# Two hi parts and the x reload moved in the middle of the MLP; in the second block one sum moved to GpSimd and the rotations set apart between heads

## The reference

```python
    # end of the first block (4096 hidden features)
    h = _rmsnorm(x, ln_mlp_g[l])
    x = x + jnp.square(jax.nn.relu(h @ w_mlp_up[l])) @ w_mlp_down[l]

    # second block
    h = x @ w_in
    x_q, x_kv, k_rope_raw, gate_a, u_pool, gate_b = jnp.split(h, splits, axis=-1)
    y_a = mla_branch(x_q, x_kv, k_rope_raw, ...) * jax.nn.silu(gate_a)
    y_b = pool_branch(u_pool, pool_w, pool_scale) * jax.nn.silu(gate_b)
    x = layer_norm(alpha * x + jnp.concatenate([y_a, y_b], axis=-1) @ w_out, ln_g, ln_b)

    # in mla_branch: 4 heads, 128 + 64 (rotated) features a query, latents of 512 and 256
    q = (rms_norm(x_q, q_norm_g) @ w_uq).reshape(B, S, MLA_HEADS, QK_DIM)
    q_nope, q_rope = q[..., :QK_NOPE_DIM], q[..., QK_NOPE_DIM:]
    q_rope = apply_rope(q_rope, cos[:, :, None, :], sin[:, :, None, :])
    kv = (rms_norm(x_kv, kv_norm_g) @ w_ukv).reshape(B, S, MLA_HEADS, QK_NOPE_DIM + V_HEAD_DIM)
    k_rope = apply_rope(k_rope_raw, cos, sin)
```

## Time and profile before

| what | value |
|---|---|
| three runs | 2297.06, 2299.01, 2300.14 us (median 2299.01) |
| profiled execution | 2299.54 us |
| its span, first to last instruction | 2297.7 us |
| mean granted TensorE clock | 0.995 |
| busy: TensorE / VectorE / GpSimd / ScalarE | 2235.4 / 1694.5 / 1195.4 / 837.3 us |
| DMA | 272.50 MB, mean 119 GB/s |

### The profile page before, as it was taken

The page is one execution under the profiler, slowest core; times in us unless marked ns, Lnnn a source line. Parts: engine busy times, 40 slices in busy tenths (PEclk is TensorE's granted clock), DMA queues, the critical chain, the costliest instruction groups (busy, mean ns, idle before and its releaser), DMA issues. The chain is left out here.

```text
span 2297.7 us, 29211 instructions
## 1 busy us (share of the span) xinstructions
PE 2235.4 (97%) x10722; PEld 1849.6 (80%) x10722; DVE 1694.5 (74%) x2037; ACT 837.3 (36%) x1165; POOL 1195.4 (52%) x895
## 2 busy tenths in 40 slices
PE   7999999999999999999999999899999999999998
PEld 5678888888888899787878888788888777778886
DVE  7899999986778354446587766677777866578777
ACT  4312243123334256213343333444343434344423
POOL 4136553333323266334478988998886678400140
PEclk9999999999999999999999999999999999999999
DMA  4121123633332422444234445654442212441231
GB/s 155 37 83 64 64 92 106 169 138 113 108 128 92 129 66 65 156 146 165 83 135 153 151 171 189 256 193 156 147 156 101 70 37 92 131 152 49 65 110 73
DMA packets 93733, 272.50 MB, mean 119 GB/s; under 512 B 8800, under 2 KB 25320, under 8 KB 87080
## 3 DMA queue, kind: packets, MB, share of 16 engines
q1 hardware_dynamic: 76544, 206.86, 26.8%
q10 hardware_dynamic: 17064, 63.99, 7.9%
HBM read 186.13 MB, written 83.90 MB: 118 GB/s over the span
## 5 line engine op out<-in xcount | busy, mean ns | idle before, releaser
L1247 PE MATMUL pair<-actA,w_hi 128*128 128x512 f32 x2016 | 624.5, 391 | 2.1 <-issue 2.1
L1247 PEld LDWEIGHTS pair<-actA,w_hi 128*128 128x128 f32 x2016 | 377.5, 188 | 81.4 <-ACT sq L1938 2.9
L1247 PE MATMUL pair<-actA,w_lo 128*128 128x512 f32 x1008 | 393.1, 390 | 0.0
L1066 POOL TENSOR_TENSOR pad<-pad 128x1 f32<-128x1 f32 x93 | 24.7, 266 | 585.3 <-PE pair L1247 506.4
L1585 PE MATMUL pair<-tring,wsp 128*128 128x512 f32 x1344 | 307.4, 391 | 8.1 <-issue 7.1
L1585 PEld LDWEIGHTS pair<-tring,wsp 128*128 128x128 f32 x1344 | 253.2, 189 | 62.2 <-issue 9.0
L1196 POOL TENSOR_TENSOR wsp<-wraw,wsp 128x512 fp32r<-128x512 f32 x124 | 188.8, 1523 | 75.5 <-ACT wsp L2205 75.1
L1247 PEld LDWEIGHTS pair<-actA,w_lo 128*128 128x128 f32 x1008 | 189.5, 188 | 39.8
L1070 POOL TENSOR_TENSOR w_lo<-raw,w_hi 128x1024 fp32r<-128x1024 f32 (+1 forms) x93 | 209.1, 2248 | 7.5
L1585 PE MATMUL pair<-tsp,wsp 128*128 128x512 f32 x768 | 184.2, 391 | 4.4 <-DVE tsp L2910 2.1
L2951 DVE TENSOR_TENSOR xB<-pair,xB 128x1024 f32<-128x1024 f32 x112 | 136.3, 1219 | 70.3 <-PE pair L1585 70.1
(11 more groups left out here) (454 smaller groups left out, 4530.2 us busy)
## 6 DMA issues: line engine op xcount, KB each, us to landing
wraw<-w_pair SPq DMA_DIRECT2D x41, 1024.0 KB, 6.0
raw<-w_in SPq DMA_DIRECT2D x62, 512.0 KB, 3.5
staged<-hid_d SPq DMA_DIRECT2D x56, 512.0 KB, 3.3
proj<-stage ACTq DMA_DIRECT2D x40, 512.0 KB, 2.6
hid_d<-hsum SPq DMA_DIRECT2D x16, 1024.0 KB, 5.0
gates<-proj ACTq DMA_DIRECT2D x18, 512.0 KB, 5.2
raw<-w_out SPq DMA_DIRECT2D x16, 512.0 KB, 3.5
hid_d<-hid SPq DMA_DIRECT2D x16, 512.0 KB, 2.8
```

Of the source, the lines that this page charges most:

```text
L1066: nc.gpsimd.tensor_tensor(pad[:, 0:1], pad[:, 1:2], pad[:, 1:2], ALU.add)
L1247: last = nc.tensor.matmul(pair[par][:, cols], w[:, slot, wk], x[:, cols], start=(k == 0 and i == 0), stop=(k == kt - 1 and i == 2))
```

## The change

- Middle of the MLP. `split_hi(6)` and `split_hi(7)` are taken ahead of the weight hi parts at 16.P2. Step 17 runs P2 ahead of P6. On SP the weights of step 18 are loaded right behind the reload of x, and SP waits for the landing of that reload before it loads tile 8 and the following ones. The turn of tile 8 is at the earliest that of 17.P2, tile 9 follows one product later, and the tiles after it two products apart, as before; so tiles 10 to 55 have turns one higher than before.
- Hand-over. VectorE makes the first half of T1 behind the last eviction of the MLP instead of between those of 31.P7 and 31.P3, its second half behind the final lo parts, and T2 ahead of T1's lo parts. The four sums of T3 are made by GpSimd (`third_sum`), behind the first weight sum of step 33, instead of by VectorE.
- Strip step 40. ScalarE takes the root for xkv behind the copy of 40.P6 instead of behind that of 39.P4; VectorE scales xkv behind the lo parts of xq. ScalarE loads cos and sin without waiting for the lo parts of xkv.
- Rotations. VectorE's order among the heads was: head 0, rope(0), head 1, rope(1), head 2, lo part 0, head 3, lo parts 1 and 2. It becomes: head 0, lo part 0, head 1, rope(0), head 2, rope(1), lo part 1, head 3, first key head, lo part 2. ScalarE's hi parts of the rotated rows 1 and 2 come one head later.

```diff
@@ -212,7 +212,9 @@
 RUN = [(0, p) for p in ("P1", "P5", "P2", "P6", "P3", "P7", "P4")]
-RUN += [(st, p) for st in range(1, STEPS) for p in ("P1", "P5", "P6", "P2", "P7", "P3", "P4")]
+RUN += [(st, p) for st in range(1, N_PAIR + 1) for p in ("P1", "P5", "P6", "P2", "P7", "P3", "P4")]
+RUN += [(N_PAIR + 1, p) for p in ("P1", "P5", "P2", "P6", "P7", "P3", "P4")]
+RUN += [(st, p) for st in range(N_PAIR + 2, STEPS) for p in ("P1", "P5", "P6", "P2", "P7", "P3", "P4")]
 NO = {key: i for i, key in enumerate(RUN)}
@@ -227,7 +229,7 @@
     if WEIGHT[_p][0] == "S":
-        SUM_NO[_st, _p] = len(SUM_NO) + 1
+        SUM_NO[_st, _p] = len(SUM_NO) + 1 + 4 * (NO[_st, _p] > NO[STEPS + 1, "P5"])
 SPLIT_OF = {"P1": 0, "P5": 1, "P6": 2, "P2": 3, "P7": 4, "P3": 5, "P4": 6}
@@ -297,7 +299,9 @@
         room.append(r)
-        turn.append(max(r, turn[-1] + (2 if j >= 7 else 1)) if turn else r + 2)
+        if j == 8:
+            r = max(r, NO[N_PAIR + 1, "P2"])
+        turn.append(max(r, turn[-1] + (2 if j >= 7 and j != 9 else 1)) if turn else r + 2)
     return turn, room
@@ -971,11 +975,13 @@
                     sp.dma_start(xB[:, 1:4:2, :], x_d[:, 1:4:2, :]).then_inc(x_in, 16)
+                    load_pair(N_PAIR + 2)
+                    sp.wait_ge(x_in, 16 * (NT + 6))
                 st, p = RUN[at_run - 1]
...
                 st = RUN[at_run][0]
-                if at_run == START[st] + 3 and st + 2 < ALL_STEPS:
+                if at_run == START[st] + 3 and N_PAIR < st < ALL_STEPS - 2:
                     load_pair(st + 2)
@@ -1170,6 +1176,15 @@

+            def third_sum():
+
+                pool.wait_ge(tsum_ok, T_SUMS + 4)
+                pool.wait_ge(lo_ok, 4 * NT + 4)
+                for k in range(4):
+                    nc.gpsimd.tensor_tensor(xB[:, k, HALF:S], xB[:, 4 + k, HALF:S], xB[:, k, HALF:S],
+                                            ALU.subtract).then_inc(summed, 1)
+                sums[0] += 4
+
             def last_unit_sums():
@@ -1189,6 +1204,8 @@
                     weight_sum(i + 1)
+                if i == START[STEPS + 1]:
+                    third_sum()
                 pool.wait_ge(wt_hi, i + 1)
@@ -2282,8 +2299,10 @@

-                c = ("T1", "T2", "T4", "T3").index(name)
-                act.wait_ge(tsum_ok, T_SUMS + (16 if name == "T4" else 4 * c + 4))
+                if name == "T3":
+                    act.wait_ge(summed, SUM_NO[STEPS + 1, "P5"] + 4)
+                else:
+                    act.wait_ge(tsum_ok, T_SUMS + 4 * ("T1", "T2", "T4").index(name) + 4)
                 for k in range(4):
@@ -2313,6 +2332,9 @@
                         square_out(NO[0, p])
+                if at_run == NO[N_PAIR, "P2"]:
+                    split_hi(6)
+                    split_hi(7)
                 late = START[N_PAIR + 1]
@@ -2322,7 +2344,7 @@
                 for j in range(N_SPLIT):
-                    if T_TURN[j] == at_run:
+                    if T_TURN[j] == at_run and j not in (6, 7):
                         split_hi(j)
@@ -2391,9 +2413,8 @@
                     root(("stat", "xq"), (squares_used, STAT_BASE["xq"] + 1), EPSV, rstd_q[:, :])
-                if i == NO[STEPS + 7, "P4"]:
+                if i == NO[STEPS + 8, "P6"]:
                     root(("stat", "xkv"), (squares_used, STAT_BASE["xq"] + 2), EPSV, rstd_kv[:, :])
-                if i == NO[STEPS + 8, "P6"]:
                     his(0, [xq_hi[:, g, :] for g in range(4)], [xq[:, g, :] for g in range(4)], (nrm, NT + 1))
@@ -2405,7 +2426,6 @@
                 if r == 0:
-                    act.wait_ge(lo_ok, base + 6)
                     act.wait_ge(cs_gb0_moved, 32)
@@ -2428,8 +2448,8 @@
                     park_q2(h - 1)
-                if h < 3:
-                    rope_hi(h)
+                if h != 1:
+                    rope_hi(max(h - 1, 0))
             park_q2(3)
@@ -3035,7 +3055,7 @@

-                c = ("T1", "T2", "T4", "T3").index(name)
+                c = ("T1", "T2", "T4").index(name)
                 if c == 0:
@@ -3046,7 +3066,7 @@
                     b11, b12_, b21, b22 = xB[:, k, 0:HALF], xB[:, k, HALF:S], xB[:, 4 + k, 0:HALF], xB[:, 4 + k, HALF:S]
-                    x, y = {"T1": (b12_, b11), "T2": (b22, b11), "T3": (b22, b12_), "T4": (b21, t2f[:, k, :])}[name]
+                    x, y = {"T1": (b12_, b11), "T2": (b22, b11), "T4": (b21, t2f[:, k, :])}[name]
                     V.tensor_tensor(t_full(name, k), x, y, ALU.subtract).then_inc(tsum_ok, 1)
@@ -3099,16 +3119,14 @@
                     final_lo(("P5", "P6", "P7", "P3").index(p))
-                if st == STEPS - 1 and p == "P7":
-                    t_sum("T1", (0, 1))
-            t_sum("T1", (2, 3))
+            t_sum("T1", (0, 1))
             for c in range(4, 8):
                 final_lo(c)
+            t_sum("T1", (2, 3))
+            t_sum("T2")
             t_los("T1")
-            t_sum("T2")
             t_sum("T4")
             t_los("T2")
-            t_sum("T3")
             t_los("T3")
@@ -3218,14 +3236,14 @@
             norm2([(g, xq[:, g, :]) for g in range(1, 4)], "q_norm_2", rstd_q)
-            dve.wait_ge(rstd_ok, 13)
-            norm2([(g, xkv[:, g, :]) for g in range(2)], "kv_norm_2", rstd_kv)
             add_strip(STEPS + 8, "P2")
...
                 low(base + g, xq_lo[:, g, :], xq[:, g, :], xq_hi[:, g, :])
+            dve.wait_ge(rstd_ok, 13)
+            norm2([(g, xkv[:, g, :]) for g in range(2)], "kv_norm_2", rstd_kv)
             n = FIRST["in2"]
@@ -3265,13 +3283,18 @@
                 low2(n, q2_hi, h + 1, q2st[:, h % 2, 1, :], q2st[:, h % 2, 0, :]).then_inc(unit_out[n % 2], 1)
-                if h < 2:
-                    rope(h)
-                for k in ((), (), (0,), (1, 2))[h]:
-                    rope_lo(k)
+                if h == 0:
+                    rope_lo(0)
+                elif h == 1:
+                    rope(0)
+                elif h == 2:
+                    rope(1)
+                    rope_lo(1)
             for h in range(4):
...
                 low2(n, kv_hi, h + 1, k2[:, 1, h, :], k2[:, 0, h, :]).then_inc(unit_out[n % 2], 1)
+                if h == 0:
+                    rope_lo(2)
             for u in range(4):
```

## The result

The changed kernel took 2312.52 us (median of 6 runs, 2306.31 to 2314.76) against 2300.84 us before (6 runs): ratio 1.0047, 95% interval 1.0032 to 1.0061. The change makes the kernel slower by 11.7 us; 5.7 had been forecast, and 2312.52 lies above the range's end of 2309.

The account below looks back on a forecast made before the run. TensorE, busy 97% of the span, was taken as the bound, so only its idle times counted. Terms +1.4 + 5.2 + 3.5 - 3.9 - 0.5 = +5.7 on 2299.54 gave 2305.2 us; range 2294.4 to 2309.

Parts of the forecast that it names:

- MLP middle: Steps 17 and 18: stall before 17.P6 goes, one of about 9 us comes before 17.P7; +1.4 us.
- a bound of +3: MLP middle: the most that the edits there were expected to cost, in us; the lower bound was -9.0.
- Later tiles: Tiles 10 to 55, split one product later: seven waits of 0.74 us before P4 of even steps; +5.2 us.
- Hand-over: Passage to the second block: VectorE's chain delays the start of 33.P4; +3.5 us, bounds -3.3 and +5.5.
- Strip step 40: Wait before 40.P6 and the slow matmuls behind it go; -3.9 us, bounds -4 and -1.
- Rotations: Two waits go, but the logits wait for the queries' load; -0.5 us, bounds -2.9 and +1.5.
- The first wait for q2st: Rotations: 1.2 us wait said to stay because kr's rotation still waits for its swap by DMA.
- a new wait "of up to 1": Rotations: a new wait of up to 1 us expected before the second ukv product.
- The second: Rival, later tiles: a lead of two is enough, lo parts take 1.24, term 0; 2300.0 us, chance 0.12.
- the third: Rival, hand-over: third sum is free for VectorE, 33.P4 starts 1.5 earlier; 2300.2 us, chance 0.14.
- The fourth: Rival: TensorE's new stalls cost the low clock twice more, 1.7 us each; 2308.6 us, chance 0.10.
- The first: Rival, MLP middle: 17.P7 does not wait, -9.0 instead of +1.4; 2294.8 us, chance 0.12.

Follow-up runs that it names:

- e2_hi8: Changed kernel with ScalarE's hi part of tile 8 moved ahead of the weight hi parts of turn 17.P1; 2300.98 us, ratio 1.0006 to the kernel before.
- e9_middle: Kernel before with the MLP middle edits alone, tiles from 10 on in their old turns; 2302.73 us, ratio 1.0018.
- e5_gap: Changed kernel with one added wait: GpSimd makes the sum for 18.P7 only after the lo part of tile 8; 2306.77 us, ratio 1.0030 to the kernel before.
- e3_turns: Changed kernel with tiles 10 to 55 split in their old turns, one product earlier; 2306.73 us, ratio 1.0038 to the kernel before.
- e11_rot2: Kernel before with the rotation edit alone, but rope_lo(1) behind the fourth head's lo part instead of ahead of it; 2296.61 us, ratio 0.9983.
- e14_middle2: One more execution of e9_middle, the same program, for a second trace; 2304.76 us in its one run.
- e10_open2: Kernel before with middle and strip edits, hi parts of tiles 8 to 10 early, tile 8's lo part later, GpSimd waiting for three lo parts; 2292.55 us, ratio 0.9968.
- e1_again: The changed kernel run once more, nothing altered; 2310.93 us, ratio 1.0054 to the kernel before.
- e8_rot: Kernel before with the edit of the rotations alone; 2302.06 us, ratio 1.0005.
- e4_hand: Changed kernel with the old hand-over: T3's sums on VectorE, T1's first half after 31.P7's eviction; 2309.24 us, ratio 1.0043 to the kernel before.
- e13_probe: No kernel: 80 trials of one VectorE subtraction against eight GpSimd subtractions in a row, with varied delay, TensorE idle or busy; 919.2 us span.
- e15_probe2: No kernel: 100 trials copying the GpSimd, ScalarE and VectorE chain around tile 8's lo part, quiet, with loads, or with TensorE busy; 1555.1 us span.

## Why the prediction was wrong

**MLP middle, the step that failed.** "0.62 for the weight hi part, 1.04 for the tile's, 1.93 for the lo part": the chain is the right one, e2_hi8 shows it, and where the lo part takes 1.84 or 1.85 the middle costs near what was forecast (+1.6 in e9_middle, +1.2 in e5_gap, +2.8 in e3_turns, for +1.4). In four of the six traces without an added wait the lo part took 6.74 instead, 4.8 more, the wait before 17.P7 came to 13.64 instead of 9, and the middle to +7. The slow matmuls behind the wait cost 2.5 to 2.7 in these four, where I had 1.7. That part doesn't follow the length of the stall: it is 1.5 to 3.0 in the seven traces, and the 3.0 stands behind the shorter stall of e3_turns. I had a bound of +3 there. It rested on VectorE waiting for one GpSimd instruction at a time: true of the other lo parts of the trace (median 1.93, 2.32 at most) and in both probes, and not where it mattered. The Trainium skill ("SBUF — State Buffer", SBUF: two separate sides) has whichever starts first, a VectorE instruction with two SBUF inputs or a GpSimd instruction that reads SBUF, hold the shared pair of ports for the whole instruction. The five GpSimd instructions in a row go beyond it, since four of them started after VectorE's recorded start at 1499.47. What lets VectorE lose so often in just that place is open: the moment of its request, a GpSimd without pauses, loads into SBUF and an idle TensorE were there in the probes and did not do it.

**Later tiles**: right. Six waits instead of seven (step 30's P4 does not wait), each dearer than the 0.74 of the forecast, 5.0 in all instead of 5.2; undone, 4.2 less.

**Hand-over**: the size came out right (3.6 against 3.5), and that was luck. Right was that T2's sums and T1's lo parts would pay 1.72 and that 33.P6 would wait on T2's lo parts. But the term was worked out as the delay of VectorE's chain up to the lo parts of T3 and T4, for which 33.P4 waits, with 1.10 more for four instructions. Twelve paid it, the lo parts at the end got 3.6 back, and in both traces of the changed kernel the chain ended 0.4 earlier than before, so that 33.P4 waited 0.83 and not longer than 2.04. What cost 3.6 was the wait before 33.P6 and the low clock behind it, less the old waits that went. In e3_turns and e5_gap the chain did end 2.9 later and 33.P4 waited 2.2; there the hand-over cost 4.4.

**Strip step 40**: right, -3.9 in each trace and -4.1 alone, against -3.9. But 1.6 of it is a low clock that before's trace happened to have: e9_middle and e11_rot2 have the same wait and not the low clock.

**Rotations**: wrong in sign. The first wait for q2st, which was to stay, went, and so did the other two, as forecast. I had a new wait "of up to 1" before the second ukv product; it came before the first, 4.1 to 5.5 long. I put the lo part of head 1's rotation at its own length; it meets GpSimd's w_lo, takes 3.27, and stands ahead of the lo part that frees the bank. e11_rot2 turns these two round and wins 2.9. That the logits would take any gain back was wrong as well: by the starts of equal matmuls the rotations of e11_rot2 put TensorE 2.2 us ahead there, and it kept them through the logits. Behind these 1.3 go, as in e14_middle2, which has no edit of the rotations.

**The rivals.** The second (tiles) fell with the waits on tring, the third (third sum) with T2's 1.72. The fourth had the right mechanism, low clock behind new stalls, at 2308.6, but without the long lo part. The first, that the middle opens, held for no trace of the change; e10_open2 shows what it takes. The medians of the edits undone or done alone (middle +3.2, tiles +4.2, hand-over +1.7, strip -4.1, rotations +1.8) add up to 6.8 of the 11.7. The middle alone mixes short and long lo parts; with the +7.2 of the long ones in its place the sum is 10.8. Each is uncertain by some 2 to 3 us, the five together by some 5, so whether the parts cost more together than alone stays open.

## What to carry to other kernels

Where a stall is removed, follow what was queued behind it on every engine. Here the wait before 17.P6 came back before 17.P7, those of the rotations before the first product of ukv, and the one before 33.P4 ahead of it, before 33.P6, each time because the instruction that TensorE needed stood behind other work; only the one before 40.P6 went for good. Move what TensorE waits for first ahead of what only prepares later work: in e2_hi8 (a tile's hi part ahead of weight hi parts) that was worth 10 us against e1_again, in e11_rot2 (the lo part that frees a bank ahead of a rotation's) about 5 against e8_rot. And where VectorE must get in beside a GpSimd that has a long run ready, a wait on GpSimd can cost nothing and save 4 us (e5_gap). A term that rests on one trace carries that execution's clock with it: at two places of this kernel the same stall of 2.0 to 2.1 us was followed by the low clock in some traces and not in others.

## What the runs showed of the hardware

- A VectorE instruction with two inputs in SBUF was kept out through five GpSimd instructions in a row (6.73 to 6.74 us in four traces, 1.84 to 1.85 in two of the same order), with the requests alike within 0.06 us. 180 trials outside the kernel, 100 of them with the same three engines and places, never showed it.
- With TensorE idle GpSimd's instructions followed each other at 1.22 us, beside a running TensorE at 1.25 (in the changed kernel 1498.97 to 1503.86 for four of them, against 1479.33 to 1480.58 for one; the same two medians in e13_probe and e15_probe2).
- Behind the same wait before 40.P6 (2.09 to 2.10 us) the granted clock fell to 1.2 GHz in three of five traces, and 24 matmuls took about 7.3 us instead of 5.69; behind the old wait before 33.P4 (2.00 to 2.04) it fell in e4_hand and e8_rot and not in before's trace.
